# Stick-breaking attention and HGRN2 step: value products gathered from two steps to four, with five weight buffers

## What is computed

```
z = einsum('bthd,bshd->bhts', q, k) * 64 ** -0.5
mask = k_pos[None, :] < q_pos[:, None]
log_fail = where(mask, log_sigmoid(-z), 0)
after = cumsum(log_fail, axis=3, reverse=True) - log_fail
a = where(mask, exp(log_sigmoid(z) + after), 0)
o = einsum('bhts,bshd->bthd', a, v)
```

## Time and profile before

| | us |
|---|---|
| median of 3 runs | 1099.34 |
| lowest, highest | 1097.09, 1099.53 |
| the profiled execution | 1096.95 |
| its span, first to last instruction | 1095.2 |

### The profile page before, as it was taken

How to read it: one execution, slowest core, us unless ns; L and a number is a source line. 1 busy time by engine, 2 the same in 40 slices (tenths; PEclk the granted TensorE clock), 3 DMA queues, 4 the chain that set the end, 5 groups by cost and what they waited for, 6 DMA issues and landing times.

```text
span 1095.2 us, 16749 instructions
## 1 busy us (share of the span) xinstructions
PE 1069.7 (98%) x6324; PEld 981.6 (90%) x6324; DVE 651.4 (59%) x1143; ACT 571.3 (52%) x1264; POOL 133.8 (12%) x145
## 2 busy tenths in 40 slices
PE   8999999999999999999999999999999999999995
PEld 5998779998779998779998779999999999999994
DVE  6677798387797377797377797345412221362117
ACT  5557883367883467883467884444032223252221
POOL 0001112011012011012011012001200100121220
PEclk9999999999999999999999999999999999999998
DMA  8041031132031132041131130143111111111144
GB/s 294 1 142 37 20 128 49 54 97 91 20 134 43 61 102 79 23 136 39 60 113 69 32 135 29 39 154 136 43 39 40 39 39 58 40 40 39 40 192 172
DMA packets 41487, 84.86 MB, mean 77 GB/s; under 512 B 2112, under 2 KB 22208, under 8 KB 41280
## 3 DMA queue, kind: packets, MB, share of 16 engines
q1 hardware_dynamic: 40832, 81.43, 22.3%
q10 hardware_dynamic: 576, 2.36, 0.6%
HBM read 67.27 MB, written 16.52 MB: 77 GB/s over the span
## 4 chain that ended last, share of the span: by engine, by line
PE 78%; ACT 9%; DVE 9%; issue 3%; DMA 1%; ACTq 0%; POOL 0%; DVEq 0%; SPq 0%; POOLq 0%
PE bank L673 50%; PE bank L1017 9%; DVE E L1682 3%; PE bank L810 3%; ACT E L1303 2%; ACT SPH L1315 2%; PE bank L840 2%; ACT E L1298 2%; DVE E L1686 1%; PE bank L796 1%; PE bank L683 1%; PE bank L710 1%; PE bank L914 1%; PE bank L959 1%; PE bank L981 1%
## 5 line engine op out<-in xcount | busy, mean ns | idle before, releaser
L673 PE MATMUL bank<-xh,wh 128*128 128x384 f32 x1296 | 438.8, 339 | 3.1 <-issue 2.9
L673 PE MATMUL bank<-xh,wl 128*128 128x384 f32 x1296 | 439.8, 339 | 0.0
L673 PE MATMUL bank<-xl,wh 128*128 128x384 f32 x1296 | 439.3, 339 | 0.0
L673 PEld LDWEIGHTS bank<-xh,wh 128*128 128x128 f32 x1296 | 243.5, 188 | 11.1 <-issue 9.3
L673 PEld LDWEIGHTS bank<-xh,wl 128*128 128x128 f32 x1296 | 243.6, 188 | 4.5 <-issue 2.0
L673 PEld LDWEIGHTS bank<-xl,wh 128*128 128x128 f32 x1296 | 243.5, 188 | 3.1 <-issue 0.2
L1188 ACT ACTIVATE slot<-bank,ngate 128x384 f32<-128x384 f32 x48 | 27.7, 578 | 178.0 <-PE bank L673 175.3
L1455 DVE CAST wh<-wr 128x1024 fp32r<-128x1024 f32 x64 | 43.7, 683 | 99.2 <-PE bank L673 98.1
L1460 DVE TENSOR_TENSOR wl<-wr,wh 128x1024 fp32r<-128x1024 f32 x64 | 90.8, 1419 | 1.9
L1682 DVE SCALAR_TENSOR_TENSOR E<-E,bank 128x512 f32<-128x512 f32 (+3 forms) x96 | 53.1, 553 | 47.8 <-ACT E L1303 47.6
L1315 ACT ACTIVATE SPH<-E 128x512 fp32r<-128x512 f32 (+2 forms) x80 | 45.4, 567 | 48.6 <-DVE E L1686 35.3
(11 more groups left out here) (229 smaller groups left out, 1672.8 us busy)
## 6 DMA issues: line engine op xcount, KB each, us to landing
wr<-wch SPq DMA_DIRECT2D x64, 512.0 KB, 3.6
KTc<-ckT SPq DMA_DIRECT2D x4, 2048.0 KB, 9.4
Vc<-cv SPq DMA_DIRECT2D x4, 2048.0 KB, 8.4
graw<-gated SPq DMA_DIRECT2D x8, 576.0 KB, 8.8
xres<-xT SPq DMA_DIRECT2D x1, 4608.0 KB, 14.2
yT<-yb SPq DMA_DIRECT2D x6, 576.0 KB, 3.0
xw<-xT SPq DMA_DIRECT2D x4, 768.0 KB, 11.4
okT<-kT ACTq DMA_DIRECT2D x4, 576.0 KB, 3.0
```

Of the source, the lines that this page charges most:

```text
L673: i = nc.tensor.matmul(CH[n % 2][:, 0:WIN], weights[:, k, :], rows[:, k, w * WIN:(w + 1) * WIN], start=(m == 0), stop=(m == 23))
```

## The change

The value products are no longer done for two tiles at each even step but for four tiles at steps 6, 10, 14, 18, 22 and 26: six groups of four products in a pair of heads where there were twelve of two, 24 for 48 in all. The weights that wait meanwhile get five buffers for three. Room for the two more comes from the row copies `zr`: four tiles became two (`zrows`), each of which holds two rows, at partition 0 and at partition 32; the high part of a row in `RT` is now written to the same partition, and the low part to the other of the two. Scratch tiles of the A stage (`hsq`, `hrs`) move from over Aw1 and Aw2 to over Aw3 and Aw4. The number and sizes of all operations stay.

```diff
-        zr = [take(f"zr{i}", [P, QW])[0] for i in range(4)]
-        aw_o = off[0] + 4 * QW
-        Aw = [take(f"Aw{i}", [P, QW])[0] for i in range(3)]
+        zrows = [take(f"zrows{i}", [P, QW])[0] for i in range(2)]
+        aw_o = off[0] + 3 * 4 * QW
+        Aw = [take(f"Aw{i}", [P, QW])[0] for i in range(5)]
...
+        def row_at(n):
+            return 32 * (n % 4 // 2)
+
+        def zr(n, cols):
+            return zrows[n % 2][row_at(n):row_at(n) + 1, cols]
+
+        def row_high(n, cols):
+            return RT[STEPS[n][2]][row_at(n):row_at(n) + 1, cols]
+
+        def row_low(n, cols):
+            return RT[STEPS[n][2]][32 - row_at(n):33 - row_at(n), cols]
...
-                    if n >= 4 and n % 2 == 0:
-                        wd, j, _ = STEPS[n - 4]
-                        c0 = first_col(n - 4)
-                        if n == 4:
+                    if n >= 6 and n % 4 == 2:
+
+                        if n == 6:
                             need(pe, s_oc, 3 * p)
                             pe.wait_ge(s_te, 6 * p + 3)
-                        if j == 4 * wd + 3:
-                            need(pe, s_gA, 2 * p + wd)
                         pe.wait_ge(s_a, NS * p + n - 2)
                         if diagonal(n - 3):
                             pe.wait_ge(s_am, DIAGS * p + diagonals_until(n - 3))
-                        for h in range(2):
-                            r = slice(DH * h, DH * h + DH)
-                            nc.tensor.matmul(OB[r, c0:QW], v_nat[:, j * P + DH * h:j * P + DH * h + DH],
-                                             Aw[(n - 4 + h) % 3][:, c0:QW], start=(j == 4 * wd + 3), stop=(j == 0),
-                                             skip_group_check=True).then_inc(s_av, 1)
+                        for m in range(n - 6, n - 2):
+                            wd, j, h = STEPS[m]
+                            c0, r = first_col(m), slice(DH * h, DH * h + DH)
+                            if j == 4 * wd + 3 and h == 0:
+                                need(pe, s_gA, 2 * p + wd)
+                            nc.tensor.matmul(OB[r, c0:QW], v_nat[:, j * P + DH * h:j * P + DH * h + DH], Aw[m % 5][:, c0:QW],
+                                             start=(j == 4 * wd + 3), stop=(j == 0), skip_group_check=True).then_inc(s_av, 1)
...
-                            nc.scalar.activation(zr[n % 4][0:1, row_col(n):QW], ZB[n % 4][0:1, row_col(n):QW], ACT.Copy)
+                            nc.scalar.activation(zr(n, slice(row_col(n), QW)), ZB[n % 4][0:1, row_col(n):QW], ACT.Copy)
...
-                        need(act, s_av, t - 2)
-                        if m < 2:
+                        need(act, s_av, t - 4)
+                        if m < 5:
...
-                        nc.scalar.activation(RT[STEPS[m][2]][0:1, cols], zr[m % 4][0:1, cols], ACT.Copy).then_inc(s_Sh, 1)
+                        nc.scalar.activation(row_high(m, cols), zr(m, cols), ACT.Copy).then_inc(s_Sh, 1)
...
-                V.tensor_tensor(RT[h][32:33, cols], zr[m % 4][0:1, cols], RT[h][0:1, cols].bitcast(F32),
-                                ALU.subtract).then_inc(s_Sl, 1)
+                V.tensor_tensor(row_low(m, cols), zr(m, cols), row_high(m, cols).bitcast(F32), ALU.subtract).then_inc(s_Sl, 1)
```

## The result

| | before | after |
|---|---|---|
| median, us | 1098.33 (1097.09 to 1099.53, 4 runs) | 1115.93 (1115.57 to 1116.50, 4 runs) |
| ratio, with its 95% interval | | 1.0161 (1.0143 to 1.0178): slower |
| span of the profiled execution | 1095.2 | 1114.3 |
| pair 1, first scores to the first products of the A stage (line 857, now 868) | 88.44 | 92.94 |

The forecast was +2.0 us in a range of -3.8 to +5.2 against the median of before; measured beside the kernel before it is +17.6. The four B stages are 4.24, 4.50, 4.98 and 4.73 us longer, 18.4 in all. The rest of the 19.1 us of span lies in front of the first of them, where the start-up of the profiled executions in this study differs by up to 2.2 us whatever the kernel.

The account below looks back on a forecast made before the run. Two nearly equal loops, TensorE's and that of ScalarE and VectorE, were taken to bound each B stage. +0.67 - 1.07 + 0.90 = +0.50 us a pair, +2.0 in four, gave 1099.0 us from 1096.95; range 1095.5 to 1104.5.

Parts of the forecast that it names:

- the sentence on the row copies: Row copies on ScalarE and VectorE keep count and size: nothing either way, at most some hundredths of a us.
- scores of step 6: TensorE: step 4's group gone (-0.57), but the scores already wait for the row of tile 2, so nothing is won.
- sums of step 9 (row product): TensorE: the sums wait for the low row of tile 5; the wait grows by 0.74 and the shift is 0.
- exp of tile 11: ScalarE: waits for the sums of step 11, delayed by step 10's bigger group (+0.69); about 0.67 us late.
- row product of step 25: TensorE has 1.5 us less work but needs the low row of tile 21; it can catch up only 1.07 us.
- end of the stage: B stage: +0.67 - 1.07 + 0.90 = +0.50 us a pair, +2.0 in four.
- The join: Second two tiles joining a group of four on TensorE: 0.05 us taken for each, bounds nothing to 0.36.
- the third rival: Value products on TensorE: each join costs 0.36 us, +1.12 a pair, +4.5 in all, 1103.8 us; 15%.
- idle times fall to about 24 and 6 us: Sign at the value products (line 840): 44 idle times, 11.0 us in all, fall to about 24 and 6 us.
- TensorE alone as the bound: Rival: ScalarE and VectorE can run ahead, so all 7.4 us saved on TensorE come off: 1091.9 us; 17%.
- The exp of tile 11 isn't held: Rival: that exp isn't delayed, or the 0.67 is made good before 290.10: -0.17 a pair, -0.7, 1098.6 us; 15%.
- the waits at the scores: Sign on TensorE: waits of the scores for the rows grow from 4.1 to some 10 us.

Follow-up runs that it names:

- g4_rows0: Changed kernel's groups of four and five buffers, but four row tiles all at partition 0 (keys of two streams not loaded): 1099.33 us, 1.0016 to the kernel before.
- g4_rows64: Changed kernel with the second row of each shared tile, and its low part, at partition 64 instead of 32: 1115.30 us, 1.0166 to the kernel before.
- g4_rows0_late10: Groups of four, rows at partition 0, keys of two streams not loaded, step 10's group behind step 11's sums: 1096.43 us, 0.9990 to the kernel before.
- g2_rows32_bank32: Kernel before with every row at partition 32 in four tiles, taken from partition 32 of the PSUM bank: 1134.76 us, 1.0339 to the kernel before.

## Why the prediction was wrong, step by step

**The failed step** is the sentence on the row copies: "The row copies keep count and size, the low row was written at partition 32 already (0.55 us for 384 columns); nothing either way, at most some hundredths." Count, size and duration do stay: the low row takes 0.55 us in the earlier trace rows and after. What changes is whether neighbours overlap it, and a duration doesn't show that. The price that reaches the end is 0.44 us for each of the 8 rows of a pair at 32: +3.5 a pair, +14.5 us measured alone. The range had no room for this, since the sentence gave the part no bounds of its own. Rows that bear on it were at hand: on ScalarE the two pairs of lines of line 1124 above, and on VectorE before, step 14 of pair 1 (the row is that of tile 12, the low row is line 1528):

```profile
280.98 0.30 DVE L1686 TENSOR_TENSOR E<-E,k 128x128 f32<-128x128 f32 x1
281.21 0.54 DVE L1522 TENSOR_TENSOR zr<-bank,zr 1x384 f32<-1x384 f32 x1
281.98 0.69 DVE L1694 TENSOR_TENSOR SPL<-E,SPH 128x512 fp32r<-128x512 f32 x1 [0.23 <-ACT SPH L1315]
282.70 0.55 DVE L1528 TENSOR_TENSOR RT<-zr,RT 1x384 fp32r<-1x384 f32 x1
```

The subtraction, at partition 0, starts 0.07 us before the end of the one ahead; the low row, at 32, starts 0.03 behind it. Every tile of the kernel before has this. Set side by side, the two would have priced a move to 32 at 0.1 us an end.

The Trainium skill has this overlap: the page "ScalarE: Activation LUTs", section "What ACT_TABLE_LOAD costs", says that back-to-back ACTIVATEs overlap by about 93 ns. The trace agrees to a thousandth (-0.094 us) as long as the start partitions stay the same. Where one changes it isn't so here (+0.012 to +0.025), and the runs decide.

**What held.** With the rows left at 0, each step can be read off g4_rows0. Shifts in pair 1, from the first scores:

| step of the ledger | predicted | g4_rows0 | after |
|---|---|---|---|
| scores of step 6 | 0 | -0.01 | +0.67 |
| sums of step 9 (row product) | 0 | -0.02 | +1.23 |
| exp of tile 11 | +0.67 | +0.65 | +1.87 |
| exp of tile 23 | +0.67 | +0.66 | +4.63 |
| end of the low row of tile 21 | +0.67 | +0.65 | +4.63 |
| row product of step 25 | +0.67 - 1.07 = -0.40 | -0.42 | +3.56 |
| end of the stage | +0.50 | +0.51 | +4.50 |

The last column is the same sum with one term exchanged: 4.63 - 1.07 + 0.94 = 4.50. 1.07 is by how much TensorE may catch up before it stands at step 25. The 0.94 is what the rest of the stage pays (foreseen 0.90). That limit is also where the missing 0.49 is. Groups alone bring TensorE to the row product of step 25 0.42 early, since it may use its late gain. Rows alone bring it there at +3.54, 0.50 us behind the low row. With both, the low row (+4.63) stops it at +3.56: the 0.42 can't be used, and the group of step 26 is paid in full all the same. In pairs 2 and 3 the changed kernel is 0.2 to 0.5 us longer than in pair 1, and so is g4_rows64; for that I have no cause. At step 25 of pair 1, after, TensorE, which answers to the second of the earlier trace rows:

```profile
328.95 0.50 PE L822 MATMUL bank<-RT,rows_r 128*128 128x512 f32 x1 [0.38 <-DVE RT L1539]
329.29 0.40 PE L822 MATMUL bank<-SPL,negtri_r 128*128 128x512 f32 x1
```

**The join.** The group of step 26, after, and what follows it:

```profile
332.14 0.34 PE L685 MATMUL bank<-xh,wl 128*128 128x384 f32 x1
332.41 1.94 PE L852 MATMUL bank<-Aw,v_nat 128*64 128x512 f32 x8
334.27 0.71 PE L868 MATMUL bank<-kTs,qbd 128*128 128x128 f32 x4
```

Against the group of two of before at the same place:

```profile
323.51 0.34 PE L673 MATMUL bank<-xh,wl 128*128 128x384 f32 x1
323.78 1.08 PE L840 MATMUL bank<-Aw,v_nat 128*64 128x512 f32 x4
324.79 0.71 PE L857 MATMUL bank<-kTs,qbd 128*128 128x128 f32 x4
```

From 332.14 to 334.27 it is 2.13 us, before it was 1.28 (323.51 to 324.79): 0.85 more, which is just the columns (4 x 0.21). The join costs 0.00, where 0.05 was taken and up to 0.36 left open. Hence the third rival (the second two pay in full) is out, and so is the +3.8 that the rule of the Trainium skill's page "TensorE: Matmul & The Clock Gate", "Part 3: Packing small matmuls — row/col tiling", would have given: its weight loads, of products that all use all rows, don't show between passes 0.43 us apart. The same page, "Step-by-step: what each phase is for", also allows a load into the background weight buffer to be pulled ahead; that fits these rows. The weight loader's records in the same group:

```profile
332.40 0.20 PEld L852 LDWEIGHTS bank<-Aw,v_nat 128*64 128x64 f32 x4 [0.25 <-issue]
332.89 0.14 PEld L852 LDWEIGHTS bank<-Aw,v_nat 128*64 128x64 f32 x2 [0.28 <-issue]
```

Here lies a slip in the prediction's reading of the earlier trace rows: the 44 idle times of 0.25 us stand beside weight loads, and it is the loader that is idle, also between the passes of a group (0.28), where TensorE's products run without a break. So "idle times fall to about 24 and 6 us" was no sign of anything; they stayed at 0.25 us each, 48 of them. The fixed part of a group was taken from start-to-start times and isn't touched by it.

**The other rivals.** TensorE alone as the bound (1091.9) is out: the exp of tile 11 was held, and g4_rows0 is slower than before. "The exp of tile 11 isn't held" is out as a forecast, but g4_rows0_late10 is just that case made on purpose: -0.7 foreseen, -1.2 (0.9990) measured. Of the signs named for the profile, the waits at the scores became 13.8 us and not "some 10"; in g4_rows0 they are 7.1, and 4.8 at the sums. "I am wrong if ... the exp of tile 11 keeps its place" never came up: the wrong sign was one that wasn't on the list, the start-to-start time of ScalarE's own instructions.

## What to carry to other kernels

That count, size and duration stay doesn't make a change free that only moves an operand to other partitions: look at gaps between neighbours, and give even a part priced at nothing its bounds from the nearest row, which here stood in the trace of before. Where an engine runs back to back and its other work starts at partition 0, keep small row work starting there too; if the row is needed at partition 32, span 0 to 32 with one instruction if the other partitions may be overwritten. When two loops are nearly equal in length, gain from one is worth only its slack to the other (here 1.07 us a pair), and where a block of work stands (before or behind the sums of step 11) is worth more than its size.

## What the hardware showed

- ScalarE instructions that follow each other with nothing to wait for start 0.094 us before the end of the one ahead. If one reads a memory (SBUF or PSUM) at another start partition than the engine's last read of that memory, or writes at another start than its last write, it starts 0.012 to 0.025 us behind the end instead: 0.11 to 0.12 us at each such change. On VectorE the two gaps are -0.08 and +0.03. This held in all 14 traces, also where both neighbours start at 0 (g2_rows32_bank32) and, the other way, where a neighbour that starts at 64 is overlapped. All changes here are between 0 and 32 or 64; two instructions that both start at 32 or 64 in all they read and write never follow each other, so that such a pair overlaps is what the rule says and no run shows.
- 33 partitions from 0 cost no more than one: 0.58 us for 33x512 where 1x512 took 0.57, and the gaps stay.
- New weights behind running fp32 products of 64 columns of the array cost nothing between passes of 512 columns (0.43 us apart, half of the 0.85 that 512 columns cost in both passes).
